# A decoder layer on one core: the opening by feature halves of the row tiles, the first block's four tiles side by side

## What is computed

```python
u = rms_norm(h, norm_mix_g[l])
z = u @ w_in[l]                       # 1024 -> 4608 + 2048 features
xa = causal_depthwise_conv(z[..., :D_LRU], conv_w[l], conv_b[l])
ha = rg_lru(xa, ...) * jax.nn.gelu(ya)
hb = multiscale_pool(xb, ...)
merged = gates[..., :d] * (ha @ w_up_a[l]) + gates[..., d:] * (hb @ w_up_b[l])
h = h + merged @ w_out[l]
```

## Time and profile before

| | us |
|---|---|
| median of 3 runs | 887.32 (887.18 to 887.77) |
| span of the profiled execution | 884.2 |
| PE busy | 837.3 (95%) |
| DVE busy | 342.1 (39%) |
| ACT busy | 272.0 (31%) |
| POOL busy | 82.0 (9%) |
| granted TensorE clock, mean | 0.984 |

### The profile page before, as it was taken

How to read it: one execution, slowest core, us unless ns; L and a number is a source line. 1 busy time by engine, 2 the same in 40 slices (tenths; PEclk the granted TensorE clock), 3 DMA queues, 4 the chain that set the end, 5 groups by cost and what they waited for, 6 DMA issues and landing times.

```text
span 884.2 us, 10342 instructions
## 1 busy us (share of the span) xinstructions
PE 837.3 (95%) x4281; PEld 528.8 (60%) x4281; DVE 342.1 (39%) x478; ACT 272.0 (31%) x397; POOL 82.0 (9%) x61
## 2 busy tenths in 40 slices
PE   4999999999999999899999999988898898999996
PEld 4888888787888888436535354352352352533685
DVE  6899549962652616511020120101100101015865
ACT  7666347733332236202010100101001001002777
POOL 3436370000000000000000000000000000001000
PEclk9999999999999999999999999999899999999998
DMA  9222222211525764999999999999999999998902
GB/s 261 95 94 96 95 96 96 96 49 50 188 96 210 293 258 180 357 422 421 398 429 427 429 425 427 427 428 428 427 428 428 427 425 431 427 421 347 356 2 95
DMA packets 45334, 253.85 MB, mean 287 GB/s; under 512 B 8868, under 2 KB 9960, under 8 KB 31976
## 3 DMA queue, kind: packets, MB, share of 16 engines
q1 hardware_dynamic: 42696, 248.21, 69.2%
q0 software_dynamic: 2304, 4.20, 1.2%
q10 hardware_dynamic: 288, 0.79, 0.2%
HBM read 246.89 MB, written 10.49 MB: 291 GB/s over the span
## 4 chain that ended last, share of the span: by engine, by line
PE 73%; DMA 16%; DVE 4%; ACT 2%; SPq 2%; issue 2%; DVEq 0%; ACTq 0%
PE bank L1434 72%; DMA ring<-in_w_down_e_dram 15%; PE bank L1647 1%; DVE ring L1121 1%; DVE ring L1101 1%; DMA ring<-in_w_in_dram 1%; ACT ring_rounded L405 1%; SPq L522 1%; DMA ring<-in_w_up_b_dram 1%; SPq L517 0%; PE bank L1740 0%; PE bank L1499 0%; ACT L1024 0%; ACT ring L778 0%; DVE pick L1228 0%
## 5 line engine op out<-in xcount | busy, mean ns | idle before, releaser
L1434 PE MATMUL bank<-ring_rounded,ring_rounded 128*128 128x512 f32 (+1 forms) x696 | 244.7, 389 | 0.1
L1434 PE MATMUL bank<-r_rounded,ring_rounded 128*128 128x512 f32 (+1 forms) x744 | 234.4, 389 | 0.8 <-DVE ring_rounded L1059 0.8
L1434 PEld LDWEIGHTS bank<-r_rounded,ring_rounded 128*128 128x128 f32 x744 | 138.9, 188 | 30.7 <-DVE ring_rounded L1059 1.0
L1434 PEld LDWEIGHTS bank<-ring_rounded,ring_rounded 128*128 128x128 f32 x696 | 130.5, 188 | 27.5 <-issue 0.7
L1434 PE MATMUL bank<-ring,gain 128*64 128x512 f32 x472 | 118.0, 603 | 8.3 <-issue 8.2
L1434 PE MATMUL bank<-ring,hT 128*64 128x512 f32 x400 | 113.7, 627 | 6.5 <-DMA ring<-in_w_down_e_dram 6.5
L1434 PE MATMUL bank<-ring,junk 128*64 128x512 f32 x472 | 115.4, 592 | 0.0
L1434 PEld LDWEIGHTS bank<-ring,gain 128*64 128x64 f32 x472 | 35.9, 138 | 75.4 <-issue 72.4
L1434 PEld LDWEIGHTS bank<-ring,junk 128*64 128x64 f32 x472 | 37.4, 137 | 71.6 <-issue 71.5
L717 POOL DMA_INDIRECT expert_rows<-r,row_i x16 | 16.6, 1035 | 669.4 <-DVE r L1321 669.4
L923 ACT ACTIVATE r<-bank,factor 128x512 f32<-128x512 f32 x16 | 11.0, 688 | 216.6 <-PE bank L1434 216.6
(11 more groups left out here) (217 smaller groups left out, 760.6 us busy)
## 6 DMA issues: line engine op xcount, KB each, us to landing
ring<-in_w_up_e_dram SPq DMA_DIRECT2D x29, 2048.0 KB, 29.4
ring<-in_w_gate_e_dram SPq DMA_DIRECT2D x24, 2048.0 KB, 28.0
ring<-in_w_down_e_dram SPq DMA_DIRECT2D x22, 2048.0 KB, 32.3
ring<-in_w_in_dram SPq DMA_DIRECT2D x18, 1024.0 KB, 7.3
r<-in_w_gate_e_dram SPq DMA_DIRECT2D x5, 2048.0 KB, 27.5
r<-in_w_down_e_dram SPq DMA_DIRECT2D x4, 2048.0 KB, 34.4
ring<-in_w_down_e_dram SPq DMA_DIRECT2D x7, 1024.0 KB, 21.7
ring<-in_w_up_e_dram SPq DMA_DIRECT2D x6, 1024.0 KB, 10.6
```

Of the source, the lines that this page charges most:

```text
L1434: return nc.tensor.matmul(*a, **k)
```

## The change

- The eight transposes with their copies and rests get an order of their own, `opening`, pairs (row tile, half): (0,0), (1,0), (2,0), (0,1), (1,1), (3,0), (2,1), (3,1). All still go round banks 4 to 7.
- TensorE issues the first six groups, the seven filler transposes ahead of the sixth. Then `open_products`: for the four tiles of block 0 in banks 0 to 3, the products of the high weight half (0,0) over the first 256 tokens, with 256 columns each, eight to a tile; the groups (2,1) and (3,1) are transposed behind the third and the fourth tile. Then the transpose of the small vectors, now into bank 4, and the same products over the other 256 tokens. Then the rest of each tile (`open_tile`): high (0,1), low (0,0), low (0,1), 16 products of 512 columns.
- The eleven filler transposes go. The wait for `prm_ready` moves from ahead of tile 3 to ahead of the first gate products.
- ScalarE: copies 0 and 1 (now those of (0,0) and (1,0)), norm 3, then the high half (0,0), copies 2 to 7, and the high half (0,1); before, copies 2 and 3 stood ahead of the high half (0,0). VectorE: rests 0 and 1 ahead of the normalisation of row tile 3, the other six behind it, as before; only what they belong to changes.

The core of the diff:

```diff
+    opening = [(0, 0), (1, 0), (2, 0), (0, 1), (1, 1), (3, 0), (2, 1), (3, 1)]
+    OPEN = 4
@@ scalar
             for i in range(TT):
+                if i == TT - 1:
+                    open_copy(0)
+                    open_copy(1)
                 act.wait_ge(x_in[i], 16)
                 norm(i, xin[:, i, :])
-                if i >= 2:
-                    copy_transposed(2 * i - 4, uT_high, (4, 5, 6, 7))
-                    copy_transposed(2 * i - 3, uT_high, (4, 5, 6, 7))
             split_high(act, 0, 0)
-            for q in range(2 * TT - 4, 2 * TT):
-                copy_transposed(q, uT_high, (4, 5, 6, 7))
+            for n in range(2, 2 * TT):
+                open_copy(n)
             split_high(act, 0, 1)
@@ vector
             for i in range(TT):
+                if i == TT - 1:
+                    open_split(0)
+                    open_split(1)
                 normalise(i, i, xin[:, i, :], xin[:, i, :])
-                if i >= 2:
-                    uT_split(2 * i - 4)
-                    uT_split(2 * i - 3)
-            for q in range(2 * TT - 4, 2 * TT):
-                uT_split(q)
+            for n in range(2, 2 * TT):
+                open_split(n)
             dve.wait_ge(const_ready, 7)
             dve.wait_ge(vec_psum, 1)
-            v.tensor_copy(prm[:, :], bank[3][:, 0:NV]).then_inc(prm_ready, 1)
+            v.tensor_copy(prm[:, :], bank[OPEN][:, 0:NV]).then_inc(prm_ready, 1)
@@ tensor
+            def open_transpose(n):
+                i, h = opening[n]
+                pe.wait_ge(norm_done, i + 1)
+                if n >= 4:
+                    pe.wait_ge(ut_low, n - 3)
...
-            for q in range(2 * TT):
-                if q == 2 * TT - 2:
+            for n in range(6):
+                if n == 5:
                     keep_busy(7)
-                transpose_rows(q, xin, (4, 5, 6, 7))
-            pe.wait_ge(small_in, 16 * 6)
-            nc.tensor.transpose(bank[3][:, 0:NV], vecs[0:NV, :], ident[0:NV, 0:NV]).then_inc(vec_psum, 1)
-            keep_busy(11)
-            pe.wait_ge(ut_low, 2 * TT)
+                open_transpose(n)
             def lru_gates(c):
+                if c == 0:
+                    pe.wait_ge(prm_ready, 1)
...
+            def open_products():
+                for half in range(2):
+                    at = slice(half * (S // 2), (half + 1) * (S // 2))
+                    if half == 0:
+                        pe.wait_ge(high_ready, 1)
+                        pe.wait_ge(ut_low, 2)
+                    else:
+                        pe.wait_ge(small_in, 16 * 6)
+                        pe.wait_ge(ut_low, 6)
+                        nc.tensor.transpose(bank[OPEN][:, 0:NV], vecs[0:NV, :], ident[0:NV, 0:NV]).then_inc(vec_psum, 1)
+                    for t in range(4):
+                        for k in range(4):
+                            w = high_half(0, 0)[:, k, t * P:(t + 1) * P]
+                            for x_ in (uT_high, uT_low):
+                                mm(bank[t][:, at], w, x_[:, k, at], start=(half == 0 and k == 0 and x_ is uT_high), stop=False)
+                        if half == 0 and t >= 2:
+                            open_transpose(4 + t)
+                pe.wait_ge(ut_low, 2 * TT)
+            def open_tile(t):
+                for g, part in ((1, "high"), (0, "low"), (1, "low")):
+                    if t == 0:
+                        if part == "high":
+                            pe.wait_ge(high_ready, halves.index((0, g)) + 1)
+                        else:
+                            pe.wait_ge(*lows_at(0, g))
```

More of the change, by code:

```diff
@@ L1052, in normalise, with uT_split @@
                                        op1=ALU.mult).then_inc(norm_done, 1)
-            def uT_split(q, high=uT_high, low=uT_low):
+            def uT_split(q, high, low):
                 i, h = q // 2 % TT, q % 2
@@ L1062, in _, with open_split @@
             dve.wait_ge(gain_in, 16)
+            def open_split(n):
+                i, h = opening[n]
+                dve.wait_ge(ut_ready, n + 1)
+                part = slice(4 * h, 4 * h + 4), slice(i * P, (i + 1) * P)
+                v.tensor_tensor(uT_low[:, part[0], part[1]], bank[4 + n % 4][:, :].rearrange("p (k t) -> p k t", k=4),
+                                uT_high[:, part[0], part[1]], ALU.subtract).then_inc(ut_low, 1)
             for i in range(TT):
+                if i == TT - 1:
+                    open_split(0)
+                    open_split(1)
                 normalise(i, i, xin[:, i, :], xin[:, i, :])
-                if i >= 2:
-                    uT_split(2 * i - 4)
-                    uT_split(2 * i - 3)
-            for q in range(2 * TT - 4, 2 * TT):
-                uT_split(q)
+            for n in range(2, 2 * TT):
+                open_split(n)
             dve.wait_ge(const_ready, 7)
             dve.wait_ge(vec_psum, 1)
-            v.tensor_copy(prm[:, :], bank[3][:, 0:NV]).then_inc(prm_ready, 1)
+            v.tensor_copy(prm[:, :], bank[OPEN][:, 0:NV]).then_inc(prm_ready, 1)
             dve.wait_ge(prm_ready, 1)
@@ L1436, in _ @@
             pe.wait_ge(const_ready, 2)
[L1438 to L1445, removed]
+            def open_transpose(n):
+                i, h = opening[n]
+                pe.wait_ge(norm_done, i + 1)
+                if n >= 4:
+                    pe.wait_ge(ut_low, n - 3)
                 for k in range(4):
-                    ins = nc.tensor.transpose(bank[banks[q % 4]][:, k * P:(k + 1) * P],
-                                              src[:, i % TT, (4 * h + k) * P:(4 * h + k + 1) * P], ident[:, :])
+                    ins = nc.tensor.transpose(bank[4 + n % 4][:, k * P:(k + 1) * P],
+                                              xin[:, i, (4 * h + k) * P:(4 * h + k + 1) * P], ident[:, :])
                 ins.then_inc(ut_psum, 1)
@@ L1525, in places @@
                 ins.then_inc(places_psum, 1)
+            def open_products():
[23 more added lines that the diff above has]
+                            pe.wait_ge(*lows_at(0, g))
+                    for k in range(4 * g, 4 * g + 4):
+                        w = (high_half if part == "high" else low_half)(0, g)[:, k % 4, t * P:(t + 1) * P]
+                        for x_ in (uT_high, uT_low)[0:2 if part == "high" else 1]:
+                            ins = mm(bank[t][:, :], w, x_[:, k, :], start=False, stop=(k == KD - 1 and part == "low"))
+                return ins
+            open_products()
             for t, (kind, c) in enumerate(tiles):
@@ L1530, in _ @@
                 dst = bank[t % 4][:, :]
-                if t == 3:
-                    pe.wait_ge(prm_ready, 1)
                 if t >= 4:
@@ L1539, in _ @@
                     pe.wait_ge(hb_low_ready, NB)
-                for g in range(k_tiles // 4):
+                if n == 0:
+                    ins = open_tile(t)
+                for g in range(k_tiles // 4 if n else 0):
                     for part in ("high", "low"):
```

4 lines of the change are left out of this document (added).

## The result

| | before | after |
|---|---|---|
| median, us | 887.32 | 891.41 (889.90 to 896.37, 5 runs) |
| ratio, 95% interval | | 1.0059 (1.0045 to 1.0073) |
| span of the profiled execution, us | 884.2 | 889.7 |

The changed kernel is slower by 0.59%, 5.2 us by the ratio and 4.1 us by the medians. Its profiled execution took 891.41 us with a span of 889.7: 1.7 us lie around the span, and so it was, to 0.1 us, in every later run. For the kernel before I had taken 3.1 us, by setting its span against the median; its profiled execution was probably about 886.0 long, faster than its median. So spans differ by 5.5 us and medians by 4.1, and the two are explained one after the other here. In the experiments three executions far above all others are left out of the medians: 957.82 in e2, 3432.08 in e7 and, beside e12, 1434.07 of the kernel before.

What follows compares the result with a forecast made beforehand. Bound: the ScalarE/VectorE chain up to 56.21 us, with TensorE 0.47 us from it, then TensorE. Forecast: 887.3 + 6.9 us for the late first convolution, POOL first, = 894.2; range 888.9 to 896.2.

Steps and rivals of the forecast that it cites:

- a fallen clock: TensorE's clock at 1.2 GHz after its idle time at the joint: would cost 1.8 us, nothing added for it.
- (b): VectorE's low part of `diag` starts before POOL's low half (1,0): first convolution 2.6 us late, 889.9 us; chance 0.30.
- (a): POOL's low half (1,0) takes the port before VectorE's low part of `diag`: first convolution 6.9 us late, 894.2 us; chance 0.50.
- The bound: Up to 56.21 us TensorE and the ScalarE/VectorE chain end within half a microsecond of each other; afterwards TensorE sets the time.
- short stalls: Unsized addition to TensorE's expected arrival at the joint, about 54.5 us.
- TensorE's side: Opening of block 0: first products at 16.05 us, half products to 24.9, about 1.4 us gained on TensorE.
- the joint: At 56.21 us, VectorE's low part of tile 3 releases TensorE; release expected at 58.8 us after the change.
- The late transposes: Last transposes, behind the first half products, delay the eighth ScalarE copy and high half (0,1); first convolution 2.6 us late.
- S: Start of ScalarE's high half (0,1): expected at 21.7 us, before 17.86, so 3.8 us later.
- (d): TensorE starts at a lower pace, with slow transposes for longer: S 0.75 us later; chance of over 896.2 us 0.05.
- Release late is paid in full: Any delay of the ScalarE/VectorE chain ahead of 56.21 us is paid in full; TensorE savings there give at most 0.47.
- Around the span: The 3.1 us between the span of before, 884.2, and the median 887.3, taken as the same after the change.

Runs made afterwards that it cites:

- e2: Kernel before with an unused VectorE reciprocal of about 2.2 us ahead of `diag`'s low part; 892.59 us, ratio 1.0076.
- e7: e3 with the convolution tile's low part moved ahead of the LRU's reciprocal on VectorE, its high part earlier on ScalarE; 889.54 us, ratio 1.0036.
- e12: e11 with one added wait: POOL begins its low half (1,0) only after VectorE's low part of `diag`; 888.00 us, ratio 1.0011.
- e4: Changed kernel with 26 filler transposes in TensorE's wait ahead of the gate products of tile 3; 892.45 us, ratio 1.0060.
- e11: Changed kernel with tile 3's gate products one tile later and pooling copies 2 and 3 ahead of ScalarE's wait for the square root's buffer; 891.77 us, ratio 1.0031.
- e1: Kernel before with an unused VectorE reciprocal of about 2.2 us behind `diag`'s low part, ahead of the first convolution; 890.63 us, ratio 1.0039.
- e3: Changed kernel with weight half (0,1) split early, ahead of the last two copies and rests, TensorE's order unchanged; 888.78 us, ratio 1.0029.
- e9: e3 with tile 3's gate products one tile later and pooling copies 2 and 3 ahead of ScalarE's wait for the square root's buffer; 887.09 us, ratio 0.9999.
- e5: Changed kernel with the convolution tile's low part moved ahead of the LRU's reciprocal on VectorE, its high part earlier on ScalarE; 893.09 us, ratio 1.0083.
- e6: Kernel before with the convolution tile's low part moved ahead of the LRU's reciprocal on VectorE, its high part earlier on ScalarE; 887.78 us, ratio 1.0015.
- e8: e3 with 26 filler transposes in TensorE's wait ahead of the gate products of tile 3; 888.66 us, ratio 1.0028.
- e10: Kernel before with tile 3's gate products one tile later and pooling copies 2 and 3 ahead of ScalarE's wait for the square root's buffer; 886.82 us, ratio 0.9996.

## Why the prediction was right, and where it was not

Predicted 894.2, range 888.9 to 896.2, slower 0.85; measured 891.41, slower. The mechanism and its sign hold; the number is between the two cases that I had worked out, for a reason that I had priced and then not counted. That it lies inside the range is in part luck: the range was to leave out a fallen clock, and it holds (b) with one only because it reaches up to (a).

- **The bound.** Right and shown: two chains meet at the gate products of tile 3. They meet at those of tile 0 as well, which the prediction had only as "short stalls": lightly in the kernel after (0.29 us at 36.28), for 2.49 to 3.27 us where POOL is first (e2, e4, e11). e1 delays one without touching the other and loses 3.5 us at the mark; e3 gives part of the delay back and gains; e9 and e12 take the meeting at tile 3 away and the loss goes, in e12 all but 0.11%.
- **TensorE's side.** First product 16.21 (16.05 expected), half products to 24.9 (24.9). The products ahead of the joint end issuing 0.9 us earlier than before, not 1.4: the last weight load ends at 54.83 instead of 55.74. As expected nothing of it shows in the time. The other 0.5 us went at least in part at tile 0, where the weight loads stood for 0.68 us up to 36.25; in the kernel before they had no such wait.
- **The late transposes.** Right in each step: S = 21.67 (21.7), `diag`'s low part at 28.93 (29.0), convolution 31.07 (31.2), release 58.59 (58.8).
- **The choice between (a) and (b) is the step that failed.** I gave (a), POOL first, 0.50, because POOL was 0.05 to 0.1 us ahead on paper. The profiled execution was (b): POOL's input came from a ScalarE operation that waited for its transfer until 27.38, while I had it start at 27.0 to 27.1, with the transfer landed as before, at 26.04. It was issued at the same time (20.08 against 20.05) and took 7.3 us instead of 6.0. I had treated the duration of one transfer as fixed. Where ScalarE did not wait for it (e4, e11), POOL was first by 0.14 and 0.15 us, at S + 7.1 against S + 7.3, as on paper. So the race hangs on S against the landing, and S itself moved: in the five traces with this opening it lay between 21.2 (e5) and 22.6 us (e11). In e11 it was late because TensorE's seven filler transposes took 1.70 us and those of (3, 0) 1.05, against 1.28 and 0.60 in the kernel after: this is the lower pace of (d), and there it went with (a). Case (a) is real, e4 and e11 show it at 6.6 us for the operation, the length that the prediction gives, and e4's mark is 6.8 us late where (a) had 6.9. The highest of the five runs of the kernel after, 896.37, may be (a) with more lost behind the mark; it has no profile. In e11, with the same opening, (a) came, by the times, seven times in twelve. A chance near even was right; to name either as the outcome was more than the profile could bear.
- **The clock is the term that was mis-sized.** The prediction had a price of 1.8 us if the clock fell, and added nothing. It fell, for 1.6 us. (b) with it is 887.3 + 2.4 + 1.6 = 891.3, the time measured. My ground was one stretch with 3.7 us of idle in all at clock 1.00. Its idle time lay in three pieces (0.65, 1.73 and 1.30 us), the wait at the joint in one, and it was one trace: in each of the 13 others the clock fell somewhere between 351 and 371 us. The Trainium skill (TensorE: Matmul & The Clock Gate, section HAM oscillation — how this bites in real kernels) says that waits between bursts of products bring the half clock; here waits of 3.33 and 3.21 us did, and so did one of 1.87 in e1, while 3.05 us in e2 did not. To follow the page would have been right in this case, and it does not explain e1 beside e2.
- **"Release late is paid in full."** Right in size, but the other direction, "an earlier release is gained in full", is false: e5, e6 and e7 show it. The ScalarE/VectorE chain meets TensorE at four places: the gate products of tile 0 and of tile 3, at 81 and at 91 to 96 us.
- **Around the span.** The 3.1 us were 1.8; it cancels in the median and cost nothing here, but a span alone compared with a median would have been wrong by 1.3.

**Open:** why the clock fell behind 1.87 us in e1 and not behind 2.49 and 3.05 in e2; whether it falls in most executions of the kernel after (e8's total did not confirm what its profile shows); whether the new opening makes the fall in the gather stage more frequent; and what makes the transfer of the second block later in the new opening.

## What to carry to other kernels

Before work is moved off a busy engine, look at who else meets it at the next joint: here TensorE was 95% busy and its head start of 0.9 us was worth nothing, since two copies and one split on the engine that feeds the other chain had been pushed behind its products. Where two operations that share a port start within half a microsecond of each other, fix the order with a wait (e12) before the kernel is tuned further, and give both orders as outcomes when predicting. Count a possible fall of the clock with every new TensorE wait of two to three microseconds, as a term of the sum and not as a remark: it fell behind seven of nine such waits here.

## What the runs showed of the hardware that was not expected

- The granted clock fell to 0.50 (1.2 GHz) behind seven of the nine waits of 1.87 to 3.33 us in the first 100 us that nothing filled: 1.2 us after the products had started again in the kernel after, 0.9 to 1.0 in e1, e3, e5 and e11, at the restart in e4, and 0.5 us before it, still in the wait, in e7. Each time it was back at 1.00 after 3.4 us, so the price is set by how much of these 3.4 us holds products: 1.5 to 1.6 us at the joint, the same in the gather stage, and nothing there in e2, e5, e8 and e10, where it was back before the stage began.
- The port between VectorE and GpSimd is held per operation: the loser waits out the whole of the other, 6.17 to 6.61 us for an operation of 2.23 (VectorE) or 6.26 for one of 4.60 (GpSimd). The Trainium skill (SBUF — State Buffer, section Who interferes with whom) states it as an exclusive lock, and the traces agree. What it makes of a kernel's times was new to me: a start order that hangs on 0.15 us gives two groups of times 5 us apart (e11), and they look like noise until the trace is read.
- A transfer of the same bytes, issued at the same time to 0.2 us, landed after 5.9 to 6.1 us in all five traces of the old opening and after 7.1 to 7.4 in the seven of the new one in which ScalarE waited for it, and that decides which engine has the port. No run here tests what delays it.
